# Attention values as plain fp32 products in column tiles, reversed projection triples, and blocks of activations read back one at a time

## The reference

```python
# A
s = jnp.einsum('bqhcd,bkhcd->bhcqk', q, k).astype(jnp.float32) * ATTN_SCALE
p = jax.nn.softmax(s, axis=-1)
w = p[:, :, 0] - lam * p[:, :, 1]
return jnp.einsum('bhqk,bkhe->bqhe', w.astype(v.dtype), v)
# B (sinks) and C (bias, no sink)
p = jax.nn.softmax(jnp.concatenate([s, sink], axis=-1), axis=-1)[..., :-1]
o = jnp.einsum('bngqk,bknd->bqngd', p.astype(v.dtype), v)
# before and after the attention
q, k, v = [z.reshape(b, t, C_HEADS, HEAD_DIM) for z in jnp.split(h @ w_in, 3, axis=-1)]
return o @ w_out, (k_new, v_new)
```

## Time and profile before

| | |
|---|---|
| runs | 3491.92 us median of 3 (3490.02 to 3502.86) |
| profiled execution | 3502.18 us, span 3500.6 |
| mean granted clock of TensorE | .964 |
| PE busy, DVE, ACT, POOL | 3215.5 us (92%), 1853.9 (53%), 1195.0 (34%), 428.0 (12%) |
| DVE on the subtraction Wl | 144 of mean 598 ns in C, 82.3 us; 80 of 595 ns in A and B, 46.3 us |
| DVE on vl in C | 8 of 1358 ns, 10.9 us |
| granted clock by stretch | A 332 to 426: .96; T4: .79; T5: .93; T6: .89; T7: .93; C 2002 to 2090: 1.00; T14: .95; networks: .99 and .98 |

### The profile page before, as it was taken

The page is one execution under the profiler, slowest core; times in us unless marked ns, Lnnn a source line. Parts: engine busy times, 40 slices in busy tenths (PEclk is TensorE's granted clock), DMA queues, the critical chain, the costliest instruction groups (busy, mean ns, idle before and its releaser), DMA issues. The chain is left out here.

```text
span 3500.6 us, 53118 instructions
## 1 busy us (share of the span) xinstructions
PE 3215.5 (92%) x20564; PEld 2019.7 (58%) x20758; DVE 1853.9 (53%) x3222; ACT 1195.0 (34%) x2527; POOL 428.0 (12%) x820
## 2 busy tenths in 40 slices
PE   7888896888899999999979999998989999999998
PEld 3455553445566666666545555555555666666665
DVE  4355554554655545554555555554636555555546
ACT  3355554533321222222235555554433122222121
POOL 1132222311000000000002222221110000000000
PEclk7899997989999999999999999999999999999998
DMA  9233332231422222222123443444421111111111
GB/s 355 79 105 106 86 90 61 77 115 34 123 62 67 67 66 61 61 79 87 50 84 110 134 133 126 135 135 153 132 64 46 43 49 43 43 43 38 43 43 61
DMA packets 247845, 305.16 MB, mean 87 GB/s; under 512 B 25027, under 2 KB 199607, under 8 KB 247042
## 3 DMA queue, kind: packets, MB, share of 16 engines
q1 hardware_dynamic: 217762, 191.78, 17.5%
q0 software_dynamic: 29920, 111.15, 10.5%
HBM read 265.99 MB, written 64.10 MB: 94 GB/s over the span
## 5 line engine op out<-in xcount | busy, mean ns | idle before, releaser
L96 PE MATMUL psum<-h,ffn_high 128*128 128x512 f32 (+1 forms) x2016 | 587.0, 399 | 2.8 <-ACT u L1069 2.8
L98 PE MATMUL psum<-hl,ffn_high 128*128 128x512 bf16 (+1 forms) x2016 | 553.3, 328 | 0.0
L96 PEld LDWEIGHTS psum<-h,ffn_high 128*128 128x128 f32 x2016 | 377.9, 188 | 134.7 <-issue 8.4
L100 PE MATMUL psum<-h,ffn_low 128*128 128x512 bf16 (+1 forms) x1901 | 444.1, 328 | 7.4
L86 PE MATMUL psum<-h,attC_high 128*128 128x384 f32 (+2 forms) x768 | 361.6, 471 | 23.9 <-issue 8.3
L1142 DVE TENSOR_SCALAR y<-u,cvT 128x1168 f32<-128x1168 f32 x88 | 78.1, 888 | 521.2 <-ACT u L1074 521.0
L86 PE MATMUL psum<-h,attAB_high 128*128 128x384 f32 (+2 forms) x672 | 326.2, 486 | 18.3 <-DVE attAB_low L189 8.5
L98 PEld LDWEIGHTS psum<-hl,ffn_high 128*128 128x128 bf16 x2016 | 194.9, 97 | 244.7
L96 PE MATMUL psum<-actr,ffn_high 128*128 128x512 f32 (+1 forms) x960 | 277.5, 397 | 7.5 <-DVE xT L672 7.5
L98 PE MATMUL psum<-actl,ffn_high 128*128 128x512 bf16 (+1 forms) x960 | 265.0, 330 | 0.0
L1068 ACT COPY u<-psum 128x1024 f32<-128x1024 f32 x88 | 89.3, 1015 | 511.5 <-PE psum L98 511.1
(11 more groups left out here) (470 smaller groups left out, 5921.4 us busy)
## 6 DMA issues: line engine op xcount, KB each, us to landing
raws<-in_w_up SPq DMA_DIRECT2D x66, 512.0 KB, 3.9
ada_raw<-in_ada_w SPq DMA_DIRECT2D x24, 1024.0 KB, 9.4
m_raw<-in_ada_w SPq DMA_DIRECT2D x48, 512.0 KB, 7.5
raw_C<-in_cache_c_v POOLq DMA_DIRECT2D x64, 256.0 KB, 4.0
out_ck_s<-in_cache_c_k POOLq DMA_DIRECT2D x8, 1984.0 KB, 8.9
out_cv_s<-in_cache_c_v POOLq DMA_DIRECT2D x8, 1984.0 KB, 15.0
raws<-in_w_in_odd SPq DMA_DIRECT2D x24, 512.0 KB, 12.5
raw_C<-in_cache_c_k POOLq DMA_DIRECT2D x48, 256.0 KB, 5.6
```

Of the source, the lines that this page charges most:

```text
L96: return pe.matmul(out, w, x[:, lo:hi], start=first and start, stop=last and stop, skip_group_check=True)
L98: return pe.matmul(out, top(w), xl[:, lo:hi], start=first and start, stop=last and stop, skip_group_check=True)
L100: return pe.matmul(out, wl, top(x[:, lo:hi]), start=first and start, stop=last and stop, skip_group_check=True)
```

## The change

The values product becomes a plain fp32 one in four column tiles (plain); the subtractions Wl and vl go, and the copies of W and v are plain fp32 copies whose ends are waited for directly. Ws gets a buffer of its own. In F and P the triples of odd k run in the opposite order (b, b, R). restore waits for each block k of h by itself, counted by PE after the last third of the last F tensor (h_free). F_UPTO of kind C is 6 in place of 5. The final part of the output projection, behind the tiles, keeps mm3, and the convolution networks are the same.

```diff
@@ -87,6 +87,15 @@
     pe.matmul(out, top(w), xl, start=False, stop=False, skip_group_check=True)
     return pe.matmul(out, wl, top(x), start=False, stop=stop, skip_group_check=True)
 
+def mm3_to_and_fro(pe, out, w, wl, x, xl, k, stop):
+
+    if k % 2 == 0:
+        return mm3(pe, out, w, wl, x, xl, k == 0, stop)
+    pe.matmul(out, wl, top(x), start=False, stop=False, skip_group_check=True)
+    pe.matmul(out, top(w), xl, start=False, stop=False, skip_group_check=True)
+    return pe.matmul(out, w, x, start=False, stop=stop, skip_group_check=True)
+
+
 def mm9(pe, ps, acc, w, wl, x, xl, start, stop):
 
     def one(b, which, first, last):
@@ -111,11 +120,12 @@
 
 
 
-def pair3(pe, out, v, vl, w, wl, start, stop):
-
-    pe.matmul(out, v, w, start=start, stop=False, skip_group_check=True)
-    pe.matmul(out, top(v), wl, start=False, stop=False, skip_group_check=True)
-    return pe.matmul(out, vl, w.bitcast(BF16)[:, :, 1::2], start=False, stop=stop, skip_group_check=True)
+def plain(pe, out, w, x, start, stop):
+
+    for j in range(4):
+        cols = slice(32 * j, 32 * j + 32)
+        mm = pe.matmul(out[cols], w[:, cols], x, start=start, stop=stop, skip_group_check=True)
+    return mm
 
 
 class Chain:
@@ -1266,7 +1276,7 @@
 
 
 AHEAD = {"A": 4, "B": 4, "C": 2}
-F_UPTO = {"B": 2, "C": 5}
+F_UPTO = {"B": 2, "C": 6}
 P_FROM = {"B": 6, "C": QB + 1}
 
 
@@ -1386,17 +1396,16 @@
         sw = sb("sw", [P, TOK])
         q, ql = sb("q", [P, TOK], F32R), sb("ql", [P, TOK], BF16)
         kk, kl = sb("k", [P, TOK], F32R), sb("kl", [P, TOK], BF16)
-        v, vl = sb("v", [P, TOK], F32R), sb("vl", [P, TOK], BF16)
+        v = sb("v", [P, TOK])
 
         E = sb("E", [P, 2560 if odd else 3072])
-        W, Wl = sb("W", [P, 1280], F32R), sb("Wl", [P, 1280], BF16)
+        W, Ws = sb("W", [P, 1280]), sb("Ws", [P, 640])
         actr, actl = sb("actr", [P, TOK], F32R), sb("actl", [P, TOK], BF16)
 
         raw = [sb(f"raw{s}", [P, 4, P]) if odd or s < 2 else
                E[:, 512 * s + 1024:512 * s + 1536].rearrange("p (j d) -> p j d", d=P) for s in range(4)]
         kc = [sb(f"kc{s}", [P, 512]) for s in range(4)]
         Qs, kn, vn = sb("Qs", [P, P]), sb("kn", [P, P]), sb("vn", [P, P])
-        Ws = Wl[:, :].bitcast(F32)
         early = [E[:, e:e + 512].rearrange("p (j d) -> p j d", d=P) for e in ((640, 1920) if odd else (1280,))]
         osb, osb2 = sb("osb", [P, P]), sb("osb2", [P, P])
         rtmp = sb("rtmp", [P, 2, TS]) if odd else E[:, 1792:2048].rearrange("p (j t) -> p j t", j=2)
@@ -1639,9 +1648,9 @@
 
             def restore():
 
-                ring.done(sp, cb + tiles[6][3] + len(tiles[6][2]) - 1)
-                sp.wait_ge(S.spilled, gone + 32 * 6)
                 for t in range(6):
+                    sp.wait_ge(S.h_free, 6 * odd + t + 1)
+                    sp.wait_ge(S.spilled, gone + 32 * max(t + 1, 5))
                     restored(t)
 
             def restored(t):
@@ -1853,10 +1862,12 @@
                     if T == T0 - 1 and name != "v" and b == 0:
                         h_ready(pe, S, m, k)
                     lo, hi = THIRDS[b]
-                    mm = mm3(pe, ps[:, f_bank(T, name, b), 0:hi - lo], w[:, k * P:(k + 1) * P], wl[:, k * P:(k + 1) * P],
-                             h[:, k, lo:hi], hl[:, k, lo:hi], k == 0, k == KT - 1)
+                    mm = mm3_to_and_fro(pe, ps[:, f_bank(T, name, b), 0:hi - lo], w[:, k * P:(k + 1) * P],
+                                        wl[:, k * P:(k + 1) * P], h[:, k, lo:hi], hl[:, k, lo:hi], k, k == KT - 1)
                     if k == KT - 1:
                         mm.then_inc(*((S.t_used[c % 2], 1) if b == 2 else (S.f_done, 1)))
+                    elif T == tiles[6][1] and name == tiles[6][2][-1] and b == 2 and k < 6:
+                        mm.then_inc(S.h_free, 1)
                 elif what == "VT":
                     pe.wait_ge(S.v_evac, 3 * (n + 1))
                     if not first:
@@ -1891,8 +1902,8 @@
                     if j == AHEAD[kind] and b < 2 and k == 0:
                         pe.wait_ge(S.v_rows, n + 1)
                     lo, hi = THIRDS[b]
-                    mm = mm3(pe, ps[:, i % 2, 0:hi - lo], w[:, k * P:(k + 1) * P], wl[:, k * P:(k + 1) * P],
-                             h[:, k, lo:hi], hl[:, k, lo:hi], k == 0, k == KT - 3)
+                    mm = mm3_to_and_fro(pe, ps[:, i % 2, 0:hi - lo], w[:, k * P:(k + 1) * P], wl[:, k * P:(k + 1) * P],
+                                        h[:, k, lo:hi], hl[:, k, lo:hi], k, k == KT - 3)
                     if k == KT - 3:
                         mm.then_inc(*((S.t_used[c % 2], 1) if b == 2 else (S.out_ready, 1)))
                 elif what == "S":
@@ -1961,10 +1972,10 @@
                     for j in range(nb):
                         x, y = slice(j * P, (j + 1) * P), slice((k0 + j) * P, (k0 + j + 1) * P)
                         if kind == "A":
-                            mm = mm3(pe, ps[:, 7, 0:P], W[:, x], Wl[:, x], v[:, y], vl[:, y], j == 0, j == nb - 1)
+                            mm = plain(pe, ps[:, 7, 0:P], W[:, x], v[:, y], j == 0, j == nb - 1)
                         else:
-                            both, low = (t[:, 0:2 * nb * P].rearrange("p (z x) -> p z x", z=2)[:, :, x] for t in (W, Wl))
-                            mm = pair3(pe, pair_o(kind, u).rearrange("p (z x) -> p z x", z=2), v[:, y], vl[:, y], both, low,
+                            both = W[:, 0:2 * nb * P].rearrange("p (z x) -> p z x", z=2)[:, :, x]
+                            mm = plain(pe, pair_o(kind, u).rearrange("p (z x) -> p z x", z=2), v[:, y], both,
                                        j == 0, j == nb - 1)
                     mm.then_inc(S.pv, 1)
                 elif what == "PV":
@@ -2177,7 +2188,7 @@
                 elif what == "VS":
                     act.wait_ge(S.v_rows, n + 1)
                     act.copy(vn[:, :], sw[:, SEQ:TOK])
-                    act.copy(v[:, :], sw[:, :]).then_inc(S.v_high, 1)
+                    act.copy(v[:, :], sw[:, :]).then_inc(S.v_low, 1)
                 elif what == "KR":
                     act.wait_ge(S.k_turned, n + 1)
                     act.wait_ge(S.v_turned, n + 1)
@@ -2197,10 +2208,7 @@
 
                         w_free(act, kind, T, u)
                     cols, src = probs_at(kind, T, u, p)
-                    if u < QB:
-                        act.copy(W[:, cols], src).then_inc(S.w_high, 1)
-                    else:
-                        act.copy(Ws[:, cols], src).then_inc(S.w_low, 1)
+                    act.copy((W if u < QB else Ws)[:, cols], src).then_inc(S.w_low, 1)
                 elif what == "K":
                     g, b = s[1:]
                     nk = CACHE_B[kind] * P
@@ -2323,20 +2331,10 @@
                 elif what == "CK":
                     dve.wait_ge(S.k_high, kv(*s[1:]) + 1)
                     dve.tensor_tensor(kl[:, :], F["k"][:, :], kk[:, :].bitcast(F32), ALU.subtract).then_inc(S.k_low, 1)
-                elif what == "VS":
-                    dve.wait_ge(S.v_high, n + 1)
-                    dve.tensor_tensor(vl[:, :], sw[:, :], v[:, :].bitcast(F32), ALU.subtract).then_inc(S.v_low, 1)
                 elif what == "S":
                     maxima(kind, T, s[1], s[2], width(kind, s[1]))
                 elif what == "X":
                     maxima(kind, T, s[1], 0, stream_width(kind))
-                elif what == "T":
-                    u, p = s[1:]
-                    if u >= QB:
-                        return
-                    dve.wait_ge(S.w_high, t_no(kind, T, u, p) - 2 * T)
-                    cols, src = probs_at(kind, T, u, p)
-                    dve.tensor_tensor(Wl[:, cols], src, W[:, cols].bitcast(F32), ALU.subtract).then_inc(S.w_low, 1)
                 elif what == "FA":
                     factors(kind, T, s[1])
                 elif what == "V" and kind == "A":
...
```

More of the change, by code:

```diff
@@ L2586, in __init__ @@
             "rope_in dup_in qz_zero q_evac k_evac v_evac q_high q_low")
-        (self.k_high, self.k_low, self.v_high, self.v_low, self.v_rows, self.k_rows, self.v_turned, self.k_turned) = make(
-            "k_high k_low v_high v_low v_rows k_rows v_turned k_turned")
+        (self.k_high, self.k_low, self.v_low, self.v_rows, self.k_rows, self.v_turned, self.k_turned) = make(
+            "k_high k_low v_low v_rows k_rows v_turned k_turned")
         (self.stored,) = make(
@@ L2594, in __init__ @@
             "qz scores stream_scores nmax exps probs turned")
-        (self.w_high, self.w_low, self.pv, self.od, self.od_turned, self.squares, self.ms, self.rstd) = make(
-            "w_high w_low pv od od_turned squares ms rstd")
+        (self.w_low, self.pv, self.od, self.od_turned, self.squares, self.ms, self.rstd) = make(
+            "w_low pv od od_turned squares ms rstd")
         (self.o_rows, self.o_turned, self.act_high, self.act_low, self.out_ready, self.out_evac) = make(
@@ L2599, in __init__ @@
```

(4 more changed lines are left out.)

## The result

The changed kernel takes 3454.98 us, the median of four runs (3451.45 to 3457.8), against 3495.13 in the four runs of the kernel before: a ratio of .9883, interval .986 to .9906, or 33 to 49 us less. The forecast was 17 us less: the direction is right, the size under half.

A forecast was written before the change was run, and what follows sets the result against it. TensorE (PE) was taken to bound nearly everything, except T4. A −10, B +3, restore −6, C +3, triples −6, vl and the rest −1 gave −17 us: 3475 on the median, likeliest case 3465 to 3485, range 3450 to 3508.

The forecast's parts named there:

- 1d: Kind A tiles: without Wl on DVE, O starts .35 us earlier per unit; −10 us, bounds 0 and −28.
- 1e: Kind B tiles: waits that go −6 us, price of plain values +9, without the restore +3 in all.
- 1a: Plain values: PE's waits for Wl that go; C gains 31 us, bounds 36 and 14; B gains 9 us.
- 1c: Tile T14 of kind C: clock recovers once the waits for Wl go; −4 us, bounds 0 and −5.
- 1b: Plain values: PE pays 4.8 us per C or B tile for blocks and column-tile passage; +38 us in C.
- The rival that made it .76: Slower rival: each unit's passage into column tiles and out costs .76 us, not .3; 3514 us, chance .15.
- 2, the restore: Tile T6: blocks returned as they come free, so PE goes on 5.6 us sooner; −6 us, bounds 0 and −10.
- 3, the triples: Reversed triples in F and P: less lost in seams over 636 pairs; −6 us, bounds −18 and +19.
- larger gain: Rival: clock holds, reversed triples pay 18 us and A 15, shorter waits return 8 more; about 3450 us, chance .19.

The follow-up runs named there:

- triple_no_wait: Kernel before without the subtraction Wl: the product that read Wl reads W's upper halves, three products kept, values result wrong; .987, 45 us less than before.
- plain_only: Kernel before with only the values product made plain in column tiles; triples, restore and F_UPTO as before; .9929, 25 us less.
- the dead subtraction: Plain values alone, plus in kinds A and B a DVE subtraction of the same shape that nobody needs; 1.0001 against the kernel before.
- after_no_fro: Changed kernel with the triples of F and P in the old order throughout; .9925, 26 us less than the kernel before.

## Why the prediction was right and where it was wrong

What failed is the price of the plain values, 47 us in the sum and 30 measured. By the two attention stages of the kernel before, of triple_no_wait and of plain_only, each from one profile, the plain values part into gain and price:

```profile
97.40:889.30 791.90, 665.92 (x4641) 409.40 (x4645) 405.32 (x1040) 356.94 (x967) 185.29 (x298) 0.92 0.29 84
1779.80:2633.50 853.70, 763.09 (x5561) 485.56 (x5565) 426.33 (x978) 393.65 (x887) 158.37 (x242) 0.98 0.39 121
```

```profile
94.60:870.10 775.50, 658.49 (x4644) 405.62 (x4644) 365.28 (x960) 357.58 (x967) 185.45 (x298) 0.93 0.30 86
1765.10:2577.90 812.80, 749.27 (x5565) 480.40 (x5565) 350.32 (x834) 394.24 (x887) 158.73 (x242) 0.99 0.40 127
```

```profile
95.30:870.50 775.20, 656.94 (x5665) 388.26 (x5665) 356.58 (x954) 357.52 (x967) 184.82 (x298) 0.94 0.30 86
1762.80:2606.00 843.20, 781.54 (x6765) 462.82 (x6765) 339.59 (x826) 395.81 (x887) 158.62 (x242) 0.99 0.39 123
```

| us | gain forecast | measured | price forecast | measured |
|---|---|---|---|---|
| A and B | 16 (1d, 1e) | 16 | 9 (1e) | 0 |
| C | 35 (1a, 1c) | 41 | 38 (1b) | 30 |

- **1e, the price in B: failed.** "The price of 4.8 − 1.2 (15 blocks a tile, not 30, so 3.6) lies on the path in T5 and T7 and half in T6": +9. From triple_no_wait to plain_only B's four tiles grow by 2.5 us (307.5 to 310.0); A's shrink by 2.6, which is why the stages show none. Part of the price in B fills waits that were there. PE's wait for DVE's E ahead of the transposes, triple_no_wait and plain_only:

```profile
PE psum L1950 <- DVE E_AB L2446: 13.7, 15, 1.2
```

```profile
PE psum L1959 <- DVE E_AB L2443: 10.8, 13, 1.1
```

  I had taken only T4 for a tile that DVE paces. That DVE paces the others too is argued, not shown: the dead subtraction left that open, and B's clock differs between the two kernels (.90 and .91).
- **1b, the price in C: mis-sized.** 4.2 us a steady tile, in place of 4.8, and .5 in T15. The blocks were right (.431, forecast .436); the passage is .23 a unit and not .3: the two losses read from the earlier trace rows, .10 and .11, come near it by themselves, and the .1 added for loading was too much. The rival that made it .76 is ruled out. In T15 PE waited 1.6 us for DVE (xT and st) in the kernel without Wl and no longer does with plain values, and the clock was .98 there and 1.00 here; both hide a part of the price.
- **1a, the waits in C: right in sum, mis-sized in a tile.** Without the last stretch C gained 36 us, where 1a and 1c had 35. But a steady tile gained 4.1, where .87 of the 3.7 listed ahead of L116 and L1950 is 3.2. A listed wait is less than what it cost. Here 1.25 us are listed, yet L116 starts 1.57 us after L88, and without Wl it starts .03 after (T10 of the kernel before and of triple_no_wait):

```profile
2055.57 0.33 PE L88 MATMUL psum<-h,attC_low 128*128 128x384 bf16 x1
2057.14 0.39 PE L116 MATMUL psum<-W_C,v_C 128*128 128x256 f32 x1 [1.25 <-DVE Wl_C L2339]
```

```profile
2030.22 0.33 PE L88 MATMUL psum<-h,attC_low 128*128 128x384 bf16 x1
2030.25 0.42 PE L116 MATMUL psum<-W_C,v_C 128*128 128x256 f32 x1
```

  The idle time is counted from the modelled end of L88. Some .3 for each of T10's three waits ahead of L116 is about what was missing.
- **1c, T14: right in kind.** The clock rose (.88 for .64 in its worst 14 us, .98 for .95 over the tile), and T14 lost 4.7 us in the changed kernel. Not in the sum was the last stretch after T15, code that the change leaves alone. Its length goes with its clock: before, changed kernel, after_no_fro:

```profile
2575.72:2633.52 57.80, 46.43 (x287) 25.96 (x289) 25.18 (x25) 17.38 (x20) 0.53 (x1) 0.88 0.13 38
```

```profile
2531.08:2583.96 52.88, 41.99 (x290) 22.46 (x289) 25.18 (x25) 17.40 (x20) 0.53 (x1) 0.96 0.14 41
```

```profile
2544.03:2600.09 56.06, 45.16 (x289) 24.72 (x289) 25.17 (x25) 17.38 (x20) 0.53 (x1) 0.90 0.13 39
```

  plain_only and triple_no_wait have .97 and 52.7 there, so 5 of C's 41 us of gain are this stretch. What decides its clock stays open: after_no_fro has plain values too.
- **1d, A: right in size**, 10 forecast and 11.0 measured (T0 to T3 with plain values alone), of which 8.3 came without Wl and the rest with the plain product, where the sum had nothing. The place is O, as the dead subtraction shows. A's clock rose along with it (.95 to .97), and what that gave is not parted from it.
- **2, the restore: right**: 5 us alone, T6 4.4 to 6.3.
- **3, the triples: right alone (6, measured 7), open in company.** 22 ns a pair in place of my 9, but only some 380 of my 636 pairs stand side by side. The sum took its terms as independent, and in the steady tile of C they are not: nothing alone, .7 us with the waits gone. Over the whole run the triples came to 6 in company by one pair of runs and 15 by the other. The reason for it held: a run of R's pays once.

In all, 17 with 17 for the price and 5 for the last stretch is 39, and up to 8 more for the triples in company; measured were 33 to 49. That the terms add up so near is in part luck, as they come from single profiles. The rival "larger gain" named the time (3450), and part of its reason is borne out: A is 13 us shorter in the changed kernel, where it had 15, and the clock rose from .92 to .94 in layer 0 and from .98 to .99 in layer 1. What the clock gave outside the last stretch no run parts from the rest.

## What to carry to other kernels

Where a wait is removed, savings on the waiting engine that the wait used to swallow can come out as well, as in the steady tile of C, so price two edits together when one of them ends a wait. A busy PE is not proof that PE sets a stage's length: put a dead instruction of the same length on the other engine, and compare stretches of equal clock. It tells which engine, not how much: here the dead subtraction cost more than the real one. And before splitting a product into column tiles to have it in plain fp32, try it whole: here the columns cost the same, and the passage was saved.

## What was unexpected of the hardware

A plain fp32 product over the whole array runs at .431 us for 256 columns at a granted clock of 1.00, where 4 × 256 cycles of 2.4 GHz are .427, so with next to no loss between blocks, and .01 on entering; in column tiles the same columns cost the same plus .23 for each visit. Two fp32r products in a row lose no more than one (.030), so that turning every other triple round saves .022 a pair.
